# Second mixer: sixteen column tiles computed as eight seven-product jobs, with two PSUM banks given up by sharing

## What is computed

```
xn = rmsnorm_2(h, mix_norm_w)
proj = xn @ w_in
g_a, g_b, za, z, xbc, dt_raw = jnp.split(proj, splits, axis=-1)
y_a = gmlp_mixer(za, ...) @ w_proj_a
# mamba2_mixer
xbc = silu(causal_dwconv(xbc, conv_w, conv_b))       # 4 taps along the tokens
xs, Bm, Cm = jnp.split(xbc, [2048, 2048 + 512], axis=-1)
y = ssd_scan(xs, dt, A, Bm, Cm) + d_skip[:, None] * xs
```

## Time and profile before

| | |
|---|---|
| median of three runs | 3614.8 us (3613.01 to 3614.93) |
| the profiled execution's own time | 3614.91 us |
| its span | 3613.1 us |
| mean granted TensorE clock | 0.996 |
| TensorE busy | 3572.3 us, 99% |
| VectorE, ScalarE, POOL busy | 1612.2, 754.7, 1517.1 us |
| the stage that is changed | from 1644.8 (end of `bc`) to 1921.5 us (start of the dense part) |

### The profile page before, as it was taken

The page is one execution under the profiler, slowest core; times in us unless marked ns, Lnnn a source line. Parts: engine busy times, 40 slices in busy tenths (PEclk is TensorE's granted clock), DMA queues, the critical chain, the costliest instruction groups (busy, mean ns, idle before and its releaser), DMA issues.

```text
span 3613.1 us, 45931 instructions
## 1 busy us (share of the span) xinstructions
PE 3572.3 (99%) x19033; PEld 2900.3 (80%) x19033; DVE 1612.2 (45%) x2476; ACT 754.7 (21%) x1368; POOL 1517.1 (42%) x1264
## 2 busy tenths in 40 slices
PE   8999999999999999999999999999999999999999
PEld 7888888788888888864588888888887468758888
DVE  3221232533336322135646633688622554358851
ACT  2000152332111100012334300100102454220000
POOL 4454222005355355424685674366530111026653
PEclk9999999999999999999999999999999999999999
DMA  4232444423332232232333222233223400033322
GB/s 136 82 89 78 90 70 64 77 53 65 70 80 84 82 94 79 88 100 67 97 105 99 82 94 82 84 92 83 87 88 103 82 24 5 6 82 82 93 77 76
DMA packets 370387, 286.32 MB, mean 79 GB/s; under 512 B 11283, under 2 KB 360083, under 8 KB 370180
## 3 DMA queue, kind: packets, MB, share of 16 engines
q1 hardware_dynamic: 367876, 279.44, 29.2%
q10 hardware_dynamic: 2304, 3.95, 0.4%
HBM read 280.64 MB, written 2.72 MB: 78 GB/s over the span
## 4 chain that ended last, share of the span: by engine, by line
PE 97%; DVE 1%; ACT 1%; issue 1%; DMA 0%; SPq 0%; DVEq 0%; ACTq 0%
PE psum L618 43%; PE psum L1078 21%; PE psum L2457 4%; PE psum L1044 3%; PE psum L3501 3%; PE psum L1742 2%; PE psum L1468 2%; PE psum L4338 2%; PE psum L4074 1%; PE psum L587 1%; PE psum L3585 1%; PE psum L1583 1%; PE psum L3605 1%; PE psum L1728 1%; PE psum L3458 1%; PE psum L1707 1%
## 5 line engine op out<-in xcount | busy, mean ns | idle before, releaser
L618 PE MATMUL psum<-work 128*128 128x256 f32 (+1 forms) x2400 | 551.4, 381 | 0.0
L537 POOL TENSOR_TENSOR work<-weight_ring 128x512 f32<-128x512 f32 x132 | 163.4, 1238 | 909.1 <-PE psum L618 731.8
L618 PEld LDWEIGHTS psum<-work 128*128 128x128 f32 x2400 | 456.0, 190 | 66.0
L618 PE MATMUL psum<-work,weight_ring 128*128 128x256 f32 (+1 forms) x2080 | 481.8, 381 | 0.0
L618 PE MATMUL psum<-normalized,weight_ring 128*128 128x256 f32 (+1 forms) x2016 | 469.5, 383 | 2.7 <-DVE normalized L738 2.7
L618 PEld LDWEIGHTS psum<-work,weight_ring 128*128 128x128 f32 x2080 | 395.2, 190 | 57.2
L618 PEld LDWEIGHTS psum<-normalized,weight_ring 128*128 128x128 f32 x2016 | 384.4, 191 | 61.3 <-DVE normalized L738 4.2
L762 DVE TENSOR_TENSOR work<-work,psum 128x512 f32<-128x512 f32 (+1 forms) x100 | 68.6, 686 | 642.5 <-PE psum L618 642.5
L1078 PE MATMUL psum<-work,weight_ring 128*128 128x256 f32 x1248 | 291.4, 379 | 0.0
L1078 PE MATMUL psum<-work 128*128 128x256 f32 x1248 | 290.8, 379 | 0.0
L696 ACT ACTIVATE work<-psum 128x256 f32<-128x256 f32 (+1 forms) x100 | 38.6, 386 | 1095.5 <-PE psum L618 1095.5
(11 more groups left out here) (556 smaller groups left out, 5273.8 us busy)
## 6 DMA issues: line engine op xcount, KB each, us to landing
weight_ring<-in_w_in SPq DMA_DIRECT2D x73, 1024.0 KB, 7.7
weight_ring<-in_w_ffn_in SPq DMA_DIRECT2D x88, 512.0 KB, 5.1
weight_ring<-in_ffn_w_up SPq DMA_DIRECT2D x44, 512.0 KB, 4.8
weight_ring<-in_ffn_up SPq DMA_DIRECT2D x44, 512.0 KB, 5.1
weight_ring<-in_w_ffn_out SPq DMA_DIRECT2D x16, 1024.0 KB, 5.0
weight_ring<-in_w_out SPq DMA_DIRECT2D x12, 1024.0 KB, 5.0
work<-decay_sums SPq DMA_DIRECT2D x16, 512.0 KB, 4.2
weight_ring<-in_w_proj_b SPq DMA_DIRECT2D x8, 1024.0 KB, 5.0
```

What stands on the lines that cost most here:

```text
L537: own(pool.tensor_tensor(s1, a21, a22, ALU.add))
L618: last = pe.matmul(K.ps[:, self.BANK[m] * T:self.BANK[m] * T + self.H], left(m, p), right(pe, m, p), start=first and p == 0, stop=last_par ...
```

## The change

All sixteen tiles of `xs` become eight jobs of the seven-product form, the first of an instance `side` that holds the gated jobs too. Its four banks are 7, 2, 0 and 1. A job's two results, raw, go to banks 4 and 5: VectorE's combining steps write them to PSUM. ScalarE then makes the first tap and the bias of the convolution (`begin_act`), VectorE the other three (`taps_dve`), ScalarE the silu. Turned tiles and states now share bank 3, outputs have bank 6 alone, groups use banks 3 and 6. The last sum of the input is made in place once `bc` is done. The groups are spread over job 0, five units apart, and 42 units (`AHEAD`) precede the first pair. The weight sums of the two token-wise slots are made in two parts.

```diff
         if plan in self.by_token:
-            return self.token_sums_pool(pool, n)
+            self.token_sums_pool(pool, n)
+            return self.last_token_sums_pool(pool, n)
...
+    def three_into_dve(self, dve, j, c11):
+
+        dve.wait_ge(*self.copied(j + 1))
+        dve.wait_ge(*self.three(j + 1))
+        dve.tensor_tensor(self.part(1), self.part(0), self.half_bank(6), ALU.add)
+        dve.tensor_tensor(c11, self.part(0), self.half_bank(2), ALU.add).then_inc(self.read_three.h, 1)
...
-TILE = 16
+AHEAD = JOB + 14
...
-    ORDER = (("bc", 8), ("xs", 16))
+    ORDER = (("bc", 8),)
...
-        banks, parts = (0, 1, 2, 7), [self.u_sums + 6 * T + i * HALF_BANK for i in range(4)]
-        self.gmlp = Sevens(K, [plans["gmlp_u"], plans["gmlp_v"]], banks, self.gmlp_sums_at, parts, by_token=[plans["gmlp_v"]])
+        banks, parts = (7, 2, 0, 1), [self.u_sums + 6 * T + i * HALF_BANK for i in range(4)]
+        self.side = Sevens(K, [plans[name] for name in ("xs", "gmlp_u", "gmlp_v")], banks, self.side_sums_at, parts, by_token=[plans["gmlp_v"]])
...
-            if i - 1 < SSM_PAIRS:
-                self.spread_line(sp, i - 1)
+            if 3 <= i - 2 < SSM_PAIRS:
+                self.spread_line(sp, i - 2)
...
     def share(self, slot):
 
-        total = (len(self.tiles) - self.first["xs"] - 2) * TILE + (len(self.gmlp.jobs) + 1) * JOB
-        return -(-(slot + 1) * total // (3 * SSM_PAIRS))
+        return AHEAD - (-(slot + 1) * ((len(self.side.jobs) + 1) * JOB - AHEAD) // (3 * SSM_PAIRS))
...
+        events = dict(one=4, three=12, five=20, all=28, begin=29, open=30, taps=38, silu=46)
...
-        xs = self.first["xs"]
+        self.spent = 0
+        side = self.side_pe(pe)
         for g in range(SSM_GROUPS):
-            if g % 2 == 0:
-                for _ in self.tile_pe(pe, xs + g // 2):
-                    pass
+            self.side_until(side, 5 * (g + 1))
             self.group_pe(pe, g)
-        self.spent = 0
-        side = self.side_pe(pe, xs + 2, len(self.tiles))
+        self.side_until(side, AHEAD)
...
     def group_banks(self, g):
-        return 3 + 2 * (g % 2), 4 + 2 * (g % 2)
+        return 3, 6
...
-            pe.wait_ge(*S["copied"](g - 1))
-            pe.wait_ge(*S["masked"](g - 1))
+            pe.wait_ge(*S["copied"](g))
+            pe.wait_ge(*S["masked"](g))
...
         if j:
-            pe.wait_ge(*S["carried"](j))
+            pe.wait_ge(*S["stated"](j))
...
-        if j > 1:
-            pe.wait_ge(*S["summed"](j - 1))
+        if j:
+            pe.wait_ge(*S["summed"](j))
...
+        self.relative_pool(pool, 0)
+        G.sums_pool(pool, 0)
+        pool.wait_ge(*self.plans["bc"].done(3))
+        self.u_side.last_sum(pool, 0, KD // 2).then_inc(S["u_summed"].h, 1)
+        G.sums_pool(pool, 1)
+        G.sums_pool(pool, 2)
+        self.weight_pool(pool, 0)
+        for j in range(1, SSM_PAIRS):
             self.relative_pool(pool, j)
-            if j == 0:
-                self.u_first.last_sum(pool, 0, KD // 2).then_inc(S["u_summed"].h, 1)
+            if j <= 9:
+                G.sums_pool(pool, j + 2)
...
+    def begin_act(self, act, j):
+
+        S = self.s
+        act.wait_ge(*self.side.read_all(j + 1))
+        for i in range(2):
+            t = 2 * j + i
+            act.activation(self.A(self.xs + t * T, T), self.raw(i), ACT.Identity, scale=self.V("ssm_conv_w_2")(3 * 24 + t),
+                           bias=self.V("ssm_conv_b_2")(t)).then_inc(S["begun"].h, 1)
...
+            if kind == "three":
+                G.three_into_dve(dve, j, B(4, HALF_BANK))
+            elif kind == "five":
+                G.five_into_dve(dve, j, B(5, HALF_BANK, P, HALF_BANK))
+            else:
+                G.all_into_dve(dve, j, by(self.K.ps[:, 4 * T + HALF_BANK:5 * T + HALF_BANK], HALF_BANK))
...
+    def raw(self, i):
+        return self.K.bank(4 + i)
+
+    def taps_dve(self, dve, own, j):
+        for i in range(2):
+            t = 2 * j + i
+            x, raw = self.A(self.xs + t * T, T), self.raw(i)
+            dve.wait_ge(*self.s["begun"](t + 1))
+            for n in range(1, 4):
+                step = dve.scalar_tensor_tensor(out=x[:, n:T], in0=raw[:, 0:T - n], scalar=self.V("ssm_conv_w_2")((3 - n) * 24 + t), in1=x[:, n:T],
+                                                op0=ALU.mult, op1=ALU.add)
```

More of the change, by code:

```diff
@@ L2513, in job_ends @@
     def job_ends(self, kinds):
-        first = (len(self.tiles) - self.first["xs"] - 2) * TILE
-        out = sorted((first + j * JOB + at, kind, j) for j in range(len(self.gmlp.jobs))
-                     for kind, at in dict(one=4, three=12, five=20, all=28, open=30).items() if kind in kinds)
+        events = dict(one=4, three=12, five=20, all=28, begin=29, open=30, taps=38, silu=46)
+        skip = lambda kind, j: kind == "open" if j < 8 else kind in ("begin", "taps", "silu")
+        out = sorted((j * JOB + at, kind, j) for j in range(len(self.side.jobs)) for kind, at in events.items()
+                     if kind in kinds and not skip(kind, j) and j)
         return [(self.slot_of(unit), kind, j) for unit, kind, j in out]
@@ L2788, in scalar @@
         self.decays_act(act, 0)
-        ends, jobs = self.slot_ends(), self.job_ends(("one", "open"))
+        self.begin_act(act, 0)
+        self.xs_silu_act(act, 0)
+        ends = self.job_ends(("one", "begin", "silu", "open"))
         for slot in range(3 * SSM_PAIRS):
@@ L2954, in vector @@
         for g in range(SSM_GROUPS):
-            if g % 2 == 0:
-                self.convolve_dve(dve, own, self.first["xs"] + g // 2)
+            if g > 1:
+                self.side_dve(dve, own, "three" if g == 2 else "five", 0)
             dve.wait_ge(*S["grouped"](g + 1))
@@ L2963, in vector @@
         own.wait()
+        self.side_dve(dve, own, "all", 0)
+        self.side_dve(dve, own, "taps", 0)
         self.aged_dve(dve, 0)
-        ends, jobs = self.slot_ends(), self.job_ends(("three", "five", "all"))
+        ends = self.job_ends(("three", "five", "all", "taps"))
         for slot in range(3 * SSM_PAIRS):
@@ L2973, in vector @@
                 self.aged_dve(dve, j + 1)
-            for place in ends.get(slot, []):
-                self.convolve_dve(dve, own, place)
-            for at, kind, job in jobs:
+            for at, kind, job in ends:
                 if at == slot:
-                    self.gmlp_dve(dve, kind, job)
+                    self.side_dve(dve, own, kind, job)
             if slot % 3 == 2:
```

177 lines of the change are left out of this document (93 added, 84 removed).

## The result

| | before | after |
|---|---|---|
| median of the runs, us | 3613.91 (3610.85 to 3614.93, 4 runs) | 3594.93 (3592.01 to 3596.41, 4 runs) |
| ratio, 95% interval | | 0.9949 [0.9933, 0.9965] |
| profiled execution, us | 3614.9 | 3592.0 |
| its span, us | 3613.1 | 3590.2 |
| end of `bc` to the turning of the gated weights, us | 276.64 | 261.50 |

The change takes 0.5% off, 0.6 us more than the low end of the forecast's range allowed. The range was missed although the stage itself gained less than forecast: 15.1 us, not 16.1. What makes up the difference lies outside the stage.

A forecast was written before the change was run, and what follows sets the result against it. TensorE, busy 99% of the span, was taken as the bound: matmuls 13.1 + gaps 2.8 + clock 1.7 - new waits 1.5 = 16.1 us off 3614.9, giving 3598.8 us, range 3595.5 to 3606.5.

The forecast's parts named there:

- The base: Whole kernel: the saving was taken off the profiled execution's 3614.9 us, with the runs' median, 3614.8, called the same.
- The matmuls, 13.1: TensorE in the pairs' stage: eight times, one 12.09 us job replaces two tiles of 13.73 us, saving 13.1 us.
- The gaps, 2.8: Head of the pairs: TensorE's idle 2.28 us before the first turning and 0.52 before the first states go.
- the clock, 1.7: Around the first gap: TensorE's clock of 0.79 over 8 us returns to 1.00, saving 1.7 us.
- The margin at the head: First turning: its input is ready at 21.6 us and TensorE arrives at 23.4, a margin of 1.8 us.
- The new waits, 1.5: Pairs' loop: TensorE's new waits for late inputs cost 1.5 us in all, between 0 and 6.3.
- The link I had found, states of pair 1: States of pair 1 wait for VectorE's factors: TensorE held 0.2 us, or 0.7 with the longest ageing.
- PSUM writes and bank sharing: VectorE's combinations writing PSUM priced like its adds reading PSUM, at worst 1.5 us more a job; bank edits cost nothing.
- B: Rival: the loop paces the pairs, TensorE waiting about 0.7 us before states or outputs of nine pairs; 3603.6 us, chance 0.26.
- C: Rival: the head keeps a gap like the old, 2.8 us and 1.7 of clock; 3603.3 us, chance 0.08.
- D: Rival: POOL becomes the bound, slowed beside VectorE to 18.0 us a pair for nine pairs; 3627.0 us, chance 0.04.

The follow-up runs named there:

- late_both: The changed kernel with the last weight sums of both token-wise slots made after the products of pairs 11 and 13; 3590.79 us, ratio 0.9943.
- share_only: The kernel before with only the banks shared as in the change, old tiles kept; 3611.56 us, ratio 0.9999.
- before_again: The kernel before, run again without an edit; 3612.14 us, ratio 0.9999.
- early_side: The kernel before with eight units of side work moved ahead of the first turning; 3614.82 us, ratio 1.0007.
- after_again: The changed kernel, run again without an edit; 3595.38 us, ratio 0.9953 to the kernel before.
- shifted: The changed kernel with the turning of the gated weights done 18 times instead of once, so the third mixer starts later; 3610.16 us, ratio 0.9997.
- after_plus5: The changed kernel with the turning of the gated weights done six times instead of once; 3600.76 us, ratio 0.9967.

## Why the prediction was wrong, step by step

- **The base, the step that failed.** "16.1 us off the profiled execution's 3614.9", with the median "the same", took all that lies outside the stage for fixed, and for the low end allowed a run "1.5 us under the others". That execution had the longest third mixer of thirteen profiles, 513.22 us; the kernel's medians over 59 later runs are 3611.5 to 3612.5. The same sum off 3612 gives 3595.9, 1.0 us from the median measured. That nearness would be partly luck: the stage gave 1.0 us less than the sum, and the part outside it, which the sum held fixed, 2.0 us more (3335.5 less 3333.5 above). Three runs of 3613.0 to 3614.9 could not show the base to be high, but the trace could have warned: the third mixer has idle stretches with low clock behind them.
- **The matmuls, 13.1: somewhat too little.** late_both, without a wait, has a stage 18.07 us shorter than before; less the 4.46 us of the head (below), 13.6 are left. A pair takes 14.64 us, forecast 14.7. The formula by which the Trainium skill (TensorE: Matmul & The Clock Gate, Back-to-back issue gap) made the term 12.7 is further off; the page gives it for an isolated matmul, and a stage of back-to-back ones is another case.
- **The gaps, 2.8, and the clock, 1.7: the sum right, the reasons only in part.** Their sum is 4.5; share_only and before_again show 2.28 + 2.18 = 4.46 us of waits and no loss of clock. It was one lateness of VectorE's first factors, part of it hidden under slow matmuls. Taken as a cause of its own the gap before the turning would have misled: early_side took it away and the stage grew.
- **The margin at the head: smaller than forecast.** The first turning is reached 23.45 us after `bc` (23.4), but its silu ends at 22.2 and not 21.6. Half of that is the last combination, which starts at 17.7 and not 17.4. Another 0.2 us are ScalarE's first tap: 0.77 us on average, where I had taken its copies' 0.58.
- **The new waits, 1.5: mis-sized and misplaced.** They are 2.9 us (261.50 against late_both's 258.57), all of them at pair 11. The link I had found, states of pair 1, holds: its factors end 0.6 us before the states start. What I missed is that the change also moves the token-wise slots' last sums, from behind the product to ahead of it. I read the ageing's price off its longest row, 2.55, which was no bound: with three operations of 2.35 us back to back on POOL it was 5.96, with one 2.54.
- **PSUM writes and bank sharing.** The combinations that write PSUM cost at most 0.02 us more than those of the same step that don't, as taken. VectorE's groups in the changed kernel, 1645 to 1847:

```profile
L1156 DVE TENSOR_TENSOR psum<-work,psum 128x512 f32<-128x512 f32 x8 | 5.6, 696 | 10.6 <-PE psum L1092 10.4 <-issue 0.2
...
L1151 DVE TENSOR_TENSOR psum<-work,psum 128x256 f32<-128x256 f32 x8 | 3.4, 428 | 0.3
...
L1156 DVE TENSOR_TENSOR work<-work,psum 128x512 f32<-128x512 f32 x5 | 3.4, 678 | 2.7 <-PE psum L1058 2.7
...
L1151 DVE TENSOR_TENSOR work<-work,psum 128x256 f32<-128x256 f32 x5 | 2.1, 421 | 0.2
```

- **The rivals.** B's 0.7 us at nine pairs did not come, nor C's gap. D priced POOL's slowdown and left out VectorE's; in its weak form (one operation a pair 1.0 us longer) POOL stays at 13.3 us a pair. The Trainium skill (GPSIMD Engine Reference, Key points) holds: the taps with an operand in PSUM last 0.745 us on average beside a nearly full POOL, and only ageing, with both inputs in SBUF, is held. How long it is held is the measurement's to say.

So the steps give 13.6 + 4.5 - 2.9 = 15.1 us, and the medians say more: 19.0 beside the result, 17.1 with after_again, 16.2 and 15.4 by shifted and after_plus5 less their added work. Some 2 us of the rest belong to the change outside its stage, and the scatter of the third mixer covers what is left. **Open** is what shortens that mixer: it was 509.4 to 513.2 us in five profiles with the old tiles and 505.8 to 511.1 in eight with the new, and the waits without a releaser near 405 us are only a part of the difference.

## What to carry to other kernels

Set a sum against the median of many runs, and look in several profiles at the stretches that the change does not touch: here one of them moved by 5 us between two executions of one kernel, a third of what the change gave. Before calling the rest scatter, average it over all runs of each kernel: here 2 us of it were not. When a wait or a low clock is to be removed, ask when the next consumer's input is ready: of 4.5 us at the head of the pairs the clock accounted for nothing, since the factors were as late without it, while in early_side, where the clock fell behind the last wait, it cost all of 2.7 us. And give an operation on two SBUF inputs as bound not its longest row, but the length of what POOL may issue in a row, and one of its own lengths more; order POOL's queue so that what VectorE's work stands beside is short.

## What the chip showed that I had not expected

- A VectorE operation of 1.22 us (1024 columns, both inputs in SBUF) lasted 5.96 and 5.97 us beside three POOL operations of 2.35 us issued one behind another, and 6.25 us where two of these were halved.
- A gap of 2.28 us in TensorE's work was followed by 1.2 GHz in one execution of the kernel before and by 2.4 GHz throughout in another (8 us windows of 0.79 and 1.00); after 4.64 us of idle time the 8 us around its end had a mean of 0.59.
- The clock of one and the same kernel in the third mixer had three low stretches in one execution and six in the next, 5.0 us of TensorE's time.
- Beside writing it to SBUF, writing a VectorE result to PSUM cost next to nothing: 0.428 against 0.421 us at 256 columns, 0.696 against 0.678 at 512.
- TensorE stood still two or three times, for 0.6 to 1.8 us each, among runs of matmuls of 64 columns with nothing in the profile to release it; in seven of the eight profiles with the change it did so once less.
